# Fourier steps halved over units, first scores ahead of the last value tile, output tiles split sooner

## What is computed

```python
h = modulate(rmsnorm(x, g1), sh1, sc1);  hc = modulate(rmsnorm(xc, g1), shc1, scc1)
z = h @ w_in                      # 9 groups of 256 columns: AU AV BX BB BC CF DQ DK DV
q, k = rope(group(z, DQ)), rope(group(z, DK))       # context keys and values come from hc
p = softmax(q k^T / sqrt(32))                       # 4 heads, each with 2 maps
o = (p[0] - lam * p[1]) @ v
mix = concat([gelu(AU) * (ws @ rmsnorm(gelu(AV)) + bs),       # mixer_a
              BB * dwconv3(BC * BX),                          # mixer_b
              real(fft2(CF, over tokens and head dim)),       # mixer_c
              rmsnorm(o) * (1 - lam_init)])                   # diff_out
x = x + gt1 * (mix @ w_out);  x = x + gt2 * conv_ffn(...)
```

## Time and profile before

| | us |
|---|---|
| median of 3 runs | 2330.57 |
| profiled execution | 2327.22 |
| its span | 2325.4 |
| TensorE busy | 2177.1 |
| VectorE busy | 1288.2 |
| ScalarE busy | 1089.6 |
| GpSimd busy | 485.6 |
| attention of layer 0, units and tail | about 121 to 253 |
| attention of layer 1, units and tail | about 782 to 859 |

### The profile page before, as it was taken

The page is one execution under the profiler, slowest core; times in us unless marked ns, Lnnn a source line. Parts: engine busy times, 40 slices in busy tenths (PEclk is TensorE's granted clock), DMA queues, the critical chain, the costliest instruction groups (busy, mean ns, idle before and its releaser), DMA issues.

```text
span 2325.4 us, 44521 instructions
## 1 busy us (share of the span) xinstructions
PE 2177.1 (94%) x19132; PEld 2046.2 (88%) x19132; DVE 1288.2 (55%) x2517; ACT 1089.6 (47%) x1880; POOL 485.6 (21%) x230
## 2 busy tenths in 40 slices
PE   4989999999999889999779998999999999999998
PEld 3967889999998678898757888999999999999998
DVE  2254444344343557556454365579658897666665
ACT  3333343132234446345433444555567776555554
POOL 0201100000002211000211243158866663000000
PEclk8999989999999999999779999999999999999999
DMA  7224323434444245665123334556544445555553
GB/s 274 74 86 150 111 90 137 147 144 165 175 161 163 91 156 184 223 205 188 73 91 133 112 118 127 167 179 191 186 139 147 147 146 165 189 184 188 186 187 127
DMA packets 97285, 355.02 MB, mean 153 GB/s; under 512 B 10689, under 2 KB 11713, under 8 KB 96705
## 3 DMA queue, kind: packets, MB, share of 16 engines
q1 hardware_dynamic: 97088, 352.18, 45.7%
HBM read 351.09 MB, written 1.05 MB: 151 GB/s over the span
## 4 chain that ended last, share of the span: by engine, by line
PE 79%; DVE 6%; issue 5%; ACT 4%; DMA 3%; POOL 2%; SPq 0%; DVEq 0%; POOLq 0%; ACTq 0%
PE ps L79 74%; PE ps L84 4%; DVE TL L114 2%; ACT TH L158 2%; POOL TL L114 1%; DMA RAW<-in_wdn 1%; PE ps L107 1%; DMA RAW<-in_wada 1%; ACT SQ L155 1%; POOL SM L114 1%; DMA RAW<-in_wup 1%; DMA RAW<-in_win 0%; ACT Hh L158 0%; DVE ps L114 0%; DVE l1st L132 0%
## 5 line engine op out<-in xcount | busy, mean ns | idle before, releaser
L158 ACT ACTIVATE TH<-RAW 128x1024 fp32r<-128x1024 f32 (+1 forms) x515 | 539.8, 1049 | 445.0 <-PE ps L79 193.3
L114 DVE TENSOR_TENSOR TL<-RAW,TH 128x1024 fp32r<-128x1024 f32 (+1 forms) x339 | 418.2, 1234 | 515.3 <-ACT TH L158 515.0
L114 POOL TENSOR_TENSOR TL<-RAW,TH 128x1024 fp32r<-128x1024 f32 x176 | 422.5, 2404 | 596.8 <-ACT TH L158 596.7
L79 PE MATMUL ps<-Hh,TL 128*128 128x256 f32 x1920 | 453.4, 289 | 44.9 <-POOL TL L114 19.4
L79 PE MATMUL ps<-Hh,TH 128*128 128x256 f32 x1920 | 442.2, 283 | 0.0
L79 PE MATMUL ps<-Hl,TH 128*128 128x256 f32 x1920 | 441.4, 282 | 0.0
L79 PEld LDWEIGHTS ps<-Hh,TL 128*128 128x128 f32 x1920 | 325.9, 194 | 74.7 <-issue 29.9
L79 PE MATMUL ps<-HXh,TL 128*128 128x256 f32 x1312 | 367.9, 284 | 12.6 <-DVE TL L114 8.0
L79 PE MATMUL ps<-HXh,TH 128*128 128x256 f32 x1312 | 362.3, 280 | 0.0
L79 PE MATMUL ps<-W,TH 128*128 128x256 f32 x2048 | 361.9, 281 | 0.0
L79 PE MATMUL ps<-HXl,TH 128*128 128x256 f32 x1312 | 361.1, 279 | 0.0
(11 more groups left out here) (323 smaller groups left out, 3016.0 us busy)
## 6 DMA issues: line engine op xcount, KB each, us to landing
RAW<-in_wada SPq DMA_DIRECT2D x144, 512.0 KB, 3.6
RAW<-in_ut SPq DMA_DIRECT2D x128, 512.0 KB, 3.5
RAW<-in_v SPq DMA_DIRECT2D x128, 512.0 KB, 3.5
RAW<-in_wup SPq DMA_DIRECT2D x88, 512.0 KB, 4.4
RAW<-in_win SPq DMA_DIRECT2D x74, 512.0 KB, 3.9
RAW<-in_wdn SPq DMA_DIRECT2D x32, 512.0 KB, 4.4
RAW<-in_wout SPq DMA_DIRECT2D x24, 512.0 KB, 3.5
RAW<-in_wq SPq DMA_DIRECT2D x16, 512.0 KB, 4.0
```

What stands on the lines that cost most here:

```text
L79: return self.e.matmul(out, lhs, rhs, start=first, stop=last, skip_group_check=skip)
L114: return DRY if self.e is None else self.e.tensor_tensor(out, a, b, op)
L158: return DRY if self.e is None else self.e.activation(out, a, ACT.Copy, **kw)
```

## The change

It moves steps; no instruction of arithmetic is added or taken away.

- `WIN_FIRST` of layer 1 is 14, 15, 16, 0, 12, 13, 1, 2, 3, 17. The queries come before the second AU tile and the AV tiles.
- `fills_at` is written out. `four2` is divided into "pq" and "dft", in different units. In layer 0 tiles 10 and 11 go to units 0 and 1 and the gate tiles to units 3, 5, 7, 9, 11 and 13, with the steps of the Fourier transform in the even units between. In layer 1 tiles 10 and 11 are in units 0 and 1, and the gate tiles in units 2 to 7.
- `scores`, `softmax` and `exps` of units 0 and 1 stand ahead of value tile 17 (layer 0: between 16 and 17, after both rotations of k; layer 1: around the turns of va). VectorE's `normal` of both and the norm of va follow.
- ScalarE rounds output tile 0 before it copies the last unit's turned tile and output tile 1 before the last squares; VectorE splits output tile 0 in the last unit, tile 1 next, tile 2 before the adaLN columns.
- GpSimd splits up to tile 17 in layer 1 ahead of the root of va. SyncE loads the second context ahead of tile 17 in place of tile 12.

Cut to its core:

```diff
-WIN_FIRST = (0, 1, 2, 3, 12, 13, 14, 15, 16, 17), (14, 15, 16, 0, 1, 2, 3, 12, 13, 17)
+WIN_FIRST = (0, 1, 2, 3, 12, 13, 14, 15, 16, 17), (14, 15, 16, 0, 12, 13, 1, 2, 3, 17)
 def fills_at(l, u):
+    if l == 0:
+        return ([("mix_a", 0), ("four", 0)], [("mix_a", 1), ("four", 1)], [("four1",)], [("gate", 2, 0)], [("pq", 0, 0)],
+                [("gate", 2, 1)], [("dft", 0, 0), ("pq", 0, 1)], [("gate", 4, 0)], [("dft", 0, 1), ("pq", 1, 0)],
+                [("gate", 4, 1)], [("dft", 1, 0), ("pq", 1, 1)], [("gate", 3, 0)], [("dft", 1, 1)], [("gate", 3, 1)],
+                [], [])[u]
+    return ([("mix_a", 0), ("four", 0)], [("mix_a", 1), ("four", 1)], [("four1",), ("gate", 2, 0)],
+            [("pq", 0, 0), ("gate", 2, 1)], [("dft", 0, 0), ("pq", 0, 1), ("gate", 4, 0)], [("dft", 0, 1), ("gate", 4, 1)],
+            [("gate", 3, 0)], [("gate", 3, 1)])[u]
...
             if l:
...
-                for j in range(2):
-                    win(j, T, A, "u", l, j)
-                    rope("k", j)
+                win(0, T, A, "u", l, 0)
+                rope("k", 0)
+                win(12, T, A, "rope", l, "q", 0)
+                rope("k", 1)
+                win(13, T, A, "rope", l, "q", 1)
                 turn_rows(0, 4, (l, "vd", 0), A, "vd", l, 0)
+                rope("q", 0)
+                win(1, T, A, "u", l, 1)
+                rope("q", 1)
                 for j in range(2):
                     win(2 + j, T, A, "tr", l, "va", j)
                 for j in range(2):
+                    scores(j)
                     turn_rows(j, NTB, (l, "va", j), A, "va", l, j)
-                win(12, T, A, "rope", l, "q", 0)
-                win(13, T, A, "rope", l, "q", 1)
-                rope("q", 0)
                 win(17, 512, A, "tr", l, "vd", 1)
-                rope("q", 1)
                 turn_rows(1, 4, (l, "vd", 1), A, "vd", l, 1)
...
+                rope(*last_rope)
+                win(16, 512, A, "tr", l, "vd", 0)
                 for j in range(2):
-                    win(16 + j, 512, A, "tr", l, "vd", j)
-                rope(*last_rope)
+                    scores(j)
+                win(17, 512, A, "tr", l, "vd", 1)
                 for j in range(2):
                     turn_rows(j, 4, (l, "vd", j), A, "vd", l, j)
...
-            for n in range(2):
-                scores(n)
...
             for n, (st, qb, hd) in enumerate(units):
                 nk = 4 if st == 0 else 2
+                if n == len(units) - 1:
+                    highs(at_tile["wout", l, 0])
...
-            highs(at_tile["wout", l, 0])
+            highs(at_tile["wout", l, 1])
             stats(("o", l, 1), y.o[:, 1, 0:T], T, D, "keep", l, len(units) - 1)
-            highs(at_tile["wout", l, 1])
...
+                lows(later(("win", l, 0), 3))
+                rope("q", 0)
+                lows(later(("win", l, 12), 3))
+                rope("q", 1)
+                lows(later(("win", l, 2), 3))
+                softmax(0)
+                softmax(1)
+                va_sums()
+                lows(later(("win", l, 3), 3))
...
+                if n == len(units) - 1:
+                    lows(at_tile["wout", l, 0])
...
-            lows(at_tile["wout", l, 0])
+            lows(at_tile["wout", l, 1])
             mix_low(2)
-            lows(at_tile["wout", l, 1])
...
+            lows(at_tile["wout", l, 1] + 1)
             if l == 0:
                 columns(9)
             scales(("m2", l), l, f"n2g{l}", 4, 1)
-            lows(at_tile["wout", l, 1] + 1)
...
-            lows(at_tile["win", l, 13])
+            lows(at_tile["win", l, 17 if l else 13])
...
-            if key == ("win", 1, 12):
+            if key == ("win", 1, 17):
```

More of the change, by code:

```diff
@@ L730, in win, with scores @@
                 project(("win", l, i), h(t), t, h1, *release)
+            def scores(n):
+                st, qb, hd = units[n]
+                j, r0 = hd // 2, 64 * (hd % 2)
+                cols, k0 = (512, 0) if st == 0 else (256, 256)
+                pe.wait_ge(D, "rope_done", l, "q" if l else "k", 1)
+                for mp in range(2):
+                    o = bank(("s", l, n, mp), A, "exp", l, n, mp)
+                    r = r0 + 32 * mp
+                    last = pe.mm_at(o[:, 0:cols], y.q[r:r + 32, j, 256 * st + 128 * qb:256 * st + 128 * qb + 128],
+                                    y.k[r:r + 32, j, k0:k0 + cols], (r, 0))
+                last.then_inc(*P.mark("s", l, n))
             if l:
@@ L796, in fill @@
                         turn_rows(j, NTB, (l, "f", j), D, "f", l, j)
-                elif what[0] == "four2":
+                elif what[0] == "pq":
                     st, j = what[1:]
@@ L804, in fill @@
                     last.then_inc(*P.mark("pq", l, st, j))
+                elif what[0] == "dft":
+                    st, j = what[1:]
                     pe.wait_ge(A, "pq", l, st, j)
@@ L1284, in vd_in, with exps @@
                          ps("row", l, "vd", j)[:, :].rearrange("p (b c) -> p b c", c=128)).then_inc(*A.mark("vd", l, j))
+            def exps(n):
+                cols = 512 if units[n][0] == 0 else 256
+                i = n % 2
+                mx, sm = y.st[:, 32 + 8 * i:34 + 8 * i], y.st[:, 34 + 8 * i:36 + 8 * i]
+                act.wait_ge(D, "max", l, n)
+                for mp in range(2):
+                    act.act(y.prob[i][:, 512 * mp:512 * mp + cols], ps("s", l, n, mp)[:, 0:cols], ACT.Exp,
+                            bias=mx[:, mp:mp + 1], scale=SCALE1, accum_out=sm[:, mp:mp + 1])\
+                        .then_inc(*A.mark("exp", l, n, mp))
             if l:
@@ L1303, in scalar_program @@
                 va_in(1)
[L1304 to L1307, removed]
+                exps(0)
+                exps(1)
                 to_rows((l, "vd", 1), ("win", l, 17), 512, 1, (P, "row", l, "va", 1))
@@ L1325, in scalar_program @@
                     to_rows((l, "vd", j), ("win", l, 16 + j), 512, j, (P, "row", l, "va", j))
+                    if j == 0:
+                        exps(0)
+                        exps(1)
                 for j in range(2):
                     vd_in(j)
[L1329 to L1337 removed]
             def fill(what):
@@ L1850, in normal @@
                 dve.stt(aa, pr[1], rc[:, 1:2], aa, ALU.mult, ALU.add).then_inc(*D.mark("att", l, n))
+            if l:
+                lows(later(("win", l, 15), 3))
+                rope("k", 0)
+                lows(later(("win", l, 16), 3))
+                rope("k", 1)
+                lows(later(("win", l, 0), 3))
[7 more added lines that the diff above has]
+                lows(later(("win", l, 3), 3))
+            else:
+                va_sums()
+                last_rope = None
+                for name, z in (("q", 12), ("k", 14)):
+                    for j in range(2):
+                        lows(at_tile["win", l, z + j] + AHEAD)
+                        if last_rope:
+                            rope(*last_rope)
+                        last_rope = name, j
+                lows(at_tile["win", l, 16])
+                rope(*last_rope)
+                lows(at_tile["win", l, 17])
+                softmax(0)
+                softmax(1)
+                lows(at_tile["win", l, 17] + AHEAD)
+            normal(0)
+            normal(1)
+            dve.wait_ge(G, "root", "va", l)
+            dve.stt(fl, fl, 8.0, sv.rearrange("p (b o) -> p b o", o=1).to_broadcast([128, 4 * NTB, 64]), ALU.mult,
+                    ALU.mult).then_inc(*D.mark("va_norm", l))
             def keep(n):
@@ L1916, in mix_low @@
                     .then_inc(*D.mark("mix_low", l, k))
-            for n in range(2):
-                softmax(n)
-                normal(n)
             for n in range(len(units)):
```

53 lines of the change are left out of this document (6 added, 47 removed).

## The result

| | before | after |
|---|---|---|
| median of the runs | 2330.03 (2328.91 to 2331.71) | 2285.97 (2285.45 to 2297.85) |
| ratio, 95% interval | | 0.9834 [0.9804, 0.9863] |
| profiled execution, its span | 2327.22, 2325.4 | 2286.08, 2284.3 |

Run twice more beside the kernel before, on two chips, it gave ratios of 0.9851 and 0.9858, so 34.6 and 33.0 us.

A forecast was written before the change was run, and what follows sets the result against it. TensorE, busy 94% of the span, bounds the kernel, so only its waits and lower clock can yield time. Layer 0's 20.7 plus layer 1's 14.3 give 35.0 us off 2327.2; with 3.4 to the median, about 2296, range 2288 to 2309.

The forecast's parts named there:

- the pq copies: Layer 0's units: waits for ScalarE's copy between the Fourier steps go, hidden under a gate tile; 4.0 us gained.
- the squares with the output start: Layer 0's tail: the waits for the last squares and output tile become about 2.4 us; 0.8 gained.
- new lock wait: Layer 1's head: GpSimd's split of tile 3 blocks VectorE's rotation, delaying tile 2's split; TensorE waits 1.7 us.
- TensorE's wait there stays: Layer 1's head, tile 13: VectorE's split, held off by GpSimd's, still takes 3.41 us; TensorE waits to 762.55.
- The squares: Layer 1's units: the 1.54 us wait for head squares shrinks to about 0.3; 1.2 us gained.
- the va root: Layer 1's head, root beside tile 11's split: by the port rule 0.9 us more, by the profile row nothing; nothing taken.
- Behind unit 0's turn in layer 1: Layer 1's head: 6.14 us at granted clock 0.50 run at full clock; 3.1 us gained.
- Layer 0's tail: After the output start, 5.50 us at granted clock 0.50 run at full clock; 2.7 us gained, nought as other end.
- The lock: Rival: GpSimd's splits hold VectorE off at five uncovered meetings of 2.2 us; 2305 us, chance 0.14.
- The clock stayed low: Rival: remaining waits keep the clock low in both tails and after layer 1's head; 7.5 us, 2304, chance 0.12.
- the halving does nothing: Rival: ScalarE reaches the pq copy behind late exponentials, so dft waits anyway; 6.3 us back, 2302, chance 0.06.
- No tile of the units came too late: Rival (tiles come too late): 16 tiles in both attentions wait 2.9 us each on average; 46 us, 2342, chance 0.08.

The follow-up runs named there:

- change_third: The changed kernel once more, unaltered, on one more chip beside the version with both later edits; median 2288.26 us, ratio 0.9858 to the kernel before.
- change_again: The changed kernel with nothing edited, on the chip of the single-part kernels; median 2294.0 us, ratio 0.9851 to the kernel before.
- fourier_not_halved: The changed kernel with both Fourier steps in one unit again, at the new places; ratio 0.9905 to the kernel before, span 2297.2 us.
- gpsimd_tile10_early: The changed kernel with GpSimd splitting tile 10 before the root of va in layer 1, not after; a single execution of 2287.8 us.
- both_edits: The changed kernel with VectorE's tile 2 split before q,0's rotation and GpSimd's tile 10 split before va's root, in layer 1; ratio 0.9833 to the kernel before.
- both_edits_again: The changed kernel with both edits of layer 1's head (VectorE's tile 2 split, GpSimd's tile 10 split earlier), rerun on another chip; median 2290.64 us, ratio 0.986.
- heads_alone: The kernel before with only the new heads (scores before value tile 17, layer 1's new projection order); ratio 0.9963, span 2307.2 us.
- split_before_rotation: The changed kernel with VectorE splitting tile 2 ahead of the rotation of q,0 in layer 1; a single execution of 2288.12 us.
- tails_alone: The kernel before with only the output tiles split sooner, heads and fills as before; ratio 0.9976, span 2322.2 us.

## Why the prediction was right, and where its sizes were off

**Layer 0** held term by term. The new waits on copies in the head were forecast as 0.3 and 0.2 and are 0.25 each; 3.68 us of idle went, forecast 3.7. Tile 10 (2.2), the pq copies (4.0) and VectorE's splits (1.6) went whole. In the tail the root's wait is 0.48, forecast 0.3, and the squares with the output start 2.35, forecast 2.4: 0.7 gained, forecast 0.8. That the 2.35 is so near is in part luck, since over the nine executions with this tail this wait lies between 1.24 and 2.97. The reason given, that tile 1's load is late, is in ScalarE's rows of the kernel after; what it did not see is that VectorE's split of tile 0 now stands ahead of the last copy of the head (233.62, 1.23 us, then l0o at 234.87), so the squares would be late even without tile 1:

```profile
233.95 1.06 ACT L158 ACTIVATE TH<-RAW 128x1024 fp32r<-128x1024 f32 x1 [1.10 <-DMA RAW<-in_wout]
235.20 0.63 ACT L155 ACTIVATE SQ<-l0o 128x512 f32<-128x512 f32 x1 [0.20 <-DVE l0o L129]
```

Output tile 2 gave 1.81, forecast 1.8.

**Layer 1's head** was forecast to give 1.9, with a new lock wait of 1.7 and the old wait at the sixth tile kept (tile 2 before, tile 13 now; the forecast calls it the fifth place). It gave 3.7. The new wait is 1.35, which is 0.35 of the difference. The old one was there in change_third, whose head has 2.2 us less idle than before, and not in the kernel after and change_again (3.7 and 3.8 less): 1.0 of it. The remaining 0.4 is a size of the chain that the runs don't take apart. The step that failed is "TensorE's wait there stays": whether it stays goes by a tenth of a microsecond between two starts.

**Layer 1's units and tail** were forecast to lose 7.6 us of waits (1.9 + 2.3 + 1.2 + 2.2) and lost 5.3. The f copy and both pq copies went whole. The squares kept 0.80 against 0.3. ScalarE has the exponentials and the rounding of a tile ahead of them (810.46, 1.06 us), but so it had before (840.97, 1.05 us); new is the copy of the second Fourier step's result (810.20, 0.38 us), which the forecast left out. The output start gave 2.0 of 2.2. The missing part is 1.18 behind va and 0.45 for GpSimd's root at 818.25. The first is a term that the sum did not have: I had counted GpSimd's root of va beside VectorE, and not what GpSimd's list has behind the root.

**Row or rule.** For the va root I went by the row (nothing) and not by the rule that VectorE is held off. The row was right: the multiplication at 760.91 took 0.16 us inside the root of 759.75 to 762.29. The meetings with a 128 x 1024 subtraction went the other way: 3.40, 2.50 and 2.27 us in place of 1.23, 0.43 and 0.16, and 3.49 of GpSimd in place of 2.40. Over the twelve traces 138 tensor-tensor steps of VectorE with no input in PSUM began inside such a subtraction, with more than 0.3 us of it left. 130 of them took at least 0.15 us more than the shortest of the same form, and the other eight are the splits beside which GpSimd took 3.49 instead. Of the 826 searches for maxima (MAX8, one input) that began there none did. The rule of the Trainium skill (page "SBUF — State Buffer", section "SBUF: two separate sides") is that the first of the two to start holds the port pair for its whole instruction. Every meeting with a whole tile's subtraction agrees that one of the two is held off, and the meetings with the root on 8 columns do not. Who starts first cannot be read from the records where they lie within 0.02 us: in those eight GpSimd is recorded first, and it was GpSimd that was held off.

**The clock** was forecast as 3.9 + 2.7 + 3.1 + 1.7 = 11.4 us. In three executions of the changed kernel it is 10.8, 7.6 and 12.0 (half of what 43.80 is less 22.20, 28.51 and 19.72). Place by place:

- Behind unit 0's turn in layer 0 (3.9) the three executions with the old heads all have a stretch at 0.50 and the nine with the new heads none. This term is the certain one.
- Behind unit 0's turn in layer 1 (3.1) all three with the old heads have one too. The kernel after and change_again still have one of 3.4 us behind the 1.18 us wait (granted clock 0.69 over the stretch below), fourier_not_halved as well. There the term gave 1.4 (6.16 less 3.41, halved), and one of the signs named for being right, no stretch at 0.50 there, failed. With that wait removed, in three executions (gpsimd_tile10_early, both_edits and both_edits_again), there was none. But change_third, heads_alone and split_before_rotation had the wait and no fall, so the wait does not decide it, and three against three and none of three is too little to show that it brings the fall.

```profile
766.47:772.00 5.53, 5.53 (x46) 5.33 (x50) 2.22 (x7) 1.73 (x5) 0.00 (x0) 0.69 0.18 73
```

- Layer 0's tail (2.7) is mis-sized on average. With the old tail all three executions had a stretch at 0.50 from the output start on, 6.8 us long. With the new tail five of nine still had one there, 3.4 us long in three and 6.8 in two, and both_edits_again one of 3.4 us shortly ahead of it; the kernel after is one of the three that had none. A mean over the nine, (4 x 3.4 + 2 x 6.8) / 9 = 3.0 in place of 6.8, gives 1.9 us where 2.7 was put.
- Layer 1's tail (1.7) held: the three with the old tail have a stretch of 3.4 us at the output start, the nine with the new tail none.

The forecast drew the 2.7 from one row, that a wait of 1.85 us at 808.85 did not lower the clock. That row is not the rule. The same wait stands in heads_alone and in tails_alone, and behind it the first did 42 matmuls in 7.16 us of busy time and the second 31, with a fall of 6.8 us:

```profile
792.47:800.32 7.85, 7.16 (x42) 3.72 (x43) 2.26 (x6) 2.16 (x5) 0.00 (x0) 1.00 0.33 96
```

```profile
807.15:815.00 7.85, 7.16 (x31) 3.69 (x32) 1.47 (x4) 1.56 (x4) 0.00 (x0) 0.57 0.04 7
```

**The rivals.** The lock ate 1.35 + 1.18, and 1.0 to 1.5 at tile 13 in some executions, not 11. The clock stayed low in part, by 0 to 4 us of the 7.5. That the halving does nothing is refuted: without it there are 12.6 us more of waits. No tile of the units came too late: in the kernel after TensorE waits for no low part there.

**The total.** The waits were forecast as 23.6 and are 22.6; with the clock 35.0 was forecast, and the first block is shorter by 34.8, 30.7 and 31.3 us in the three profiled executions. That the total came out so near is partly luck: 2.3 us too much in layer 1's units and tail, 1.8 too little in its head, 1.0 of it since the wait at tile 13 did not occur. The range missed the first median, since it was made from the change alone: it allowed 2 us for falls of the clock elsewhere, where unchanged code gave 8.0 in the profiled pair, and the medians of the changed kernel on three occasions, 2285.97 to 2294.0, differ by as much.

## What to carry to other kernels

Where one engine is busy 94% of the time, sum its waits by stage and its time at the lower clock apart. Most waits repeat to 0.1 us and can be forecast one by one from the rows; here the exceptions were one behind a load (1.24 to 2.97 us) and one where two engines start within a tenth of a microsecond (none or 1.0 to 1.5 us). Falls of the clock come at much the same places of the program, but some come or stay away, and the same one lasts 6.8 us in one execution and 13.7 in another, so they are worth a chance, not a sum. A step that copies between two products belongs a whole unit before its use, since the in-order engine that copies may have a softmax ahead of it. When a step is moved past an instruction of GpSimd, look at what its list holds behind it too: a subtraction of a whole tile holds up whatever step with two inputs from SBUF VectorE begins at that moment, even one of one column.

## What the runs showed of the hardware that I had not expected

The same pair of splits goes one way or the other between executions, told above at change_third, and in all twelve it goes with what follows.

TensorE has two paces at granted clock 1.00. Rows of two matmuls of 256 columns in the kernel before, in a stretch of the one kind and of the other:

```profile
64.68 0.39 PE L79 MATMUL ps<-Hh,TL 128*128 128x256 f32 x2
64.91 0.39 PE L79 MATMUL ps<-Hh,TH 128*128 128x256 f32 x2
```

```profile
97.10 0.40 PE L79 MATMUL ps<-Hh,TL 128*128 128x256 f32 x2
97.34 0.40 PE L79 MATMUL ps<-Hh,TH 128*128 128x256 f32 x2
```

From row to row it is 0.23 and 0.24 us; over many, the median from start to start of one matmul is 113 ns in some stretches of 10 us and 117 to 118 in others, 4% apart, in every kernel, and where the slower stretches lie differs between executions. I take it to be the part of the differences that is neither wait nor clock: 1.4 us in the first block and 3.0 behind it in the pair above, and up to 17 us between other executions. What is left of the length behind the first block after idle and half/2 is 1334.6 us before, 1318.5 in change_third and 1317.6 in fourier_not_halved. Of the stretches of 10 us at full clock the slower kind (117 ns or more) makes 80 before, 38 in change_third and 28 in fourier_not_halved. What sets it the runs don't show.
